# Rounding the weight pieces on ACT in the three projections with a convolution, DVE forming the remainders

## The reference, cut to what matters

```python
def causal_short_conv(x, w):
    s = x.shape[1]
    xp = jnp.pad(x, ((0, 0), (CONV_W - 1, 0), (0, 0)))
    y = xp[:, 0:s] * w[0]
    for k in range(1, CONV_W):
        y = y + xp[:, k:k + s] * w[k]
    return y
```

## Time and profile before

| | us |
|---|---|
| median of 3 runs | 5344.36 |
| lowest, highest | 5342.21, 5353.56 |
| profiled execution, its own time | 5340.43 |
| its span | 5338.6 |
| PE busy | 4357.7 (82%) |
| PEld busy | 2946.5 (55%) |
| DVE busy | 3132.0 (59%) |
| ACT busy | 731.9 (14%) |
| POOL busy | 818.7 (15%) |
| mean granted clock of TensorE | 0.909 of full speed |

### The profile page before, as it was taken

One profiled execution on the slowest core, in us unless ns is written; L12 is line 12 of the kernel. 1 busy time (PEld: TensorE's weight loads), 2 busy tenths in 40 slices (PEclk: granted clock), 3 DMA queues, 4 the chain that ended last, 5 costly groups with the idle time before them and its releaser, 6 DMA issues. The chain is left out here.

```text
span 5338.6 us, 46516 instructions
## 1 busy us (share of the span) xinstructions
PE 4357.7 (82%) x16256; PEld 2946.5 (55%) x16256; DVE 3132.0 (59%) x5411; ACT 731.9 (14%) x1680; POOL 818.7 (15%) x756
## 2 busy tenths in 40 slices
PE   7788969787787777677978678699996789787987
PEld 3676755222222222446746446577775567576876
DVE  2344357778778775654464485555556246445774
ACT  0111111111111010110131341100001210311000
POOL 1000023434433343100020041100002000001001
PEclk9899989999999999888989779799998699588998
DMA  7212216999999999200201101122222022022222
GB/s 252 85 56 81 88 63 260 423 424 423 423 416 416 415 416 421 76 24 8 75 16 64 49 1 53 60 87 89 91 90 68 24 75 80 8 73 74 95 77 75
DMA packets 212434, 813.26 MB, mean 152 GB/s; under 512 B 20288, under 2 KB 22608, under 8 KB 146448
## 3 DMA queue, kind: packets, MB, share of 16 engines
q0 software_dynamic: 73728, 536.90, 24.2%
q1 hardware_dynamic: 137408, 267.62, 15.1%
q10 hardware_dynamic: 1104, 6.30, 0.3%
HBM read 808.67 MB, written 2.10 MB: 152 GB/s over the span
## 5 line engine op out<-in xcount | busy, mean ns | idle before, releaser
L122 DVE CAST ring_high<-ring_raw 128x2048 fp32r<-128x2048 f32 (+2 forms) x250 | 274.4, 1097 | 934.7 <-PE psum L152 864.8
L150 PE MATMUL psum<-h_features,ring_high 128*128 128x512 f32 (+3 forms) x1432 | 566.0, 395 | 56.8 <-DVE ring_low L124 25.0
L151 PE MATMUL psum<-h_features,ring_high 128*128 128x512 f32 (+3 forms) x1432 | 562.4, 393 | 0.0
L152 PE MATMUL psum<-h_features,ring_low 128*128 128x512 f32 (+3 forms) x1432 | 562.0, 392 | 0.0
L124 DVE TENSOR_TENSOR ring_low<-ring_raw,ring_high 128x2048 fp32r<-128x2048 f32 (+2 forms) x250 | 509.6, 2038 | 19.0
L150 PE MATMUL psum<-ring_high,h_features 128*128 128x512 f32 x1120 | 443.1, 396 | 59.1 <-DVE ring_low L124 45.6
L925 PE MATMUL psum<-slots_ring,evacuation_tmp 128*128 128x512 f32 x816 | 403.7, 618 | 104.8 <-DVE evacuation_tmp L1023 104.7
L151 PE MATMUL psum<-ring_low,h_features 128*128 128x512 f32 x1120 | 441.0, 394 | 0.0
L152 PE MATMUL psum<-ring_high,h_features 128*128 128x512 f32 x1120 | 440.6, 393 | 0.0
L417 POOL TENSOR_SCALAR mean_var<-mean_var 128x1 f32<-128x1 f32 (+3 forms) x43 | 10.3, 241 | 2710.2 <-DVEq L455 1500.5
L925 PE MATMUL psum<-slots_features,evacuation_tmp 128*128 128x512 f32 x612 | 302.1, 617 | 77.2 <-DVE evacuation_tmp L1023 77.0
(11 more groups left out here) (453 smaller groups left out, 7227.0 us busy)
## 6 DMA issues: line engine op xcount, KB each, us to landing
ring_raw<-in_w_in SPq DMA_DIRECT2D x94, 1024.0 KB, 5.0
ring_raw<-in_w_gate_up SPq DMA_DIRECT2D x32, 1024.0 KB, 5.1
ada_ring<-in_w_ada SPq DMA_DIRECT2D x24, 1024.0 KB, 5.9
ring_raw<-in_w_up_pairs SPq DMA_DIRECT2D x20, 1024.0 KB, 4.9
ring_raw<-in_w_down SPq DMA_DIRECT2D x33, 512.0 KB, 3.6
ring_raw<-in_w_out SPq DMA_DIRECT2D x12, 1024.0 KB, 5.0
ring_raw<-in_w_down SPq DMA_DIRECT2D x10, 1024.0 KB, 4.9
ring_raw<-in_peer_w_q SPq DMA_DIRECT2D x8, 1024.0 KB, 5.1
```

Of the source, the lines that this page charges most:

```text
L122: nc.vector.tensor_copy(high, whole)
L150: nc.tensor.matmul(out, a[0], b[0], start=start, stop=False)
L151: nc.tensor.matmul(out, a[0], b[1], start=False, stop=False)
L152: return nc.tensor.matmul(out, a[1], b[0], start=False, stop=stop)
```

## The change

In a stage that has a "conv" run, the cast of every piece but the first ones (those of `split_first`) moves from DVE to ACT. ACT waits for what DVE waited for (`wait_piece`), copies raw to high and counts `rounded[half]`; DVE waits for that and forms the remainder. On ACT both roundings for chunk c + 1 stand ahead of ACT's work on chunk c. The stages get two semaphores more, all 24 of them. Other stages split as before.

```diff
--- before.py
+++ after.py
@@ -124,19 +124,48 @@
     return nc.vector.tensor_tensor(low, whole, high.bitcast(F32), ALU.subtract)
 
 
-def split_piece(nc, core, dve, c, half, cols=PIECE):
+def piece_columns(core, c, half):
 
     if isinstance(c, int):
         if c >= len(core.plan):
-            return
-        cols = core.plan[c][1][half].shape[1] * core.plan[c][1][half].shape[2]
-    dve.wait_ge(core.landed[half], 16 * (c + 1))
+            return 0
+        return core.plan[c][1][half].shape[1] * core.plan[c][1][half].shape[2]
+    return PIECE
+
+
+def wait_piece(core, eng, c, half):
+
+    eng.wait_ge(core.landed[half], 16 * (c + 1))
     if not isinstance(c, int) or c > 0:
         if half == 0:
-            dve.wait_ge(core.used, c)
+            eng.wait_ge(core.used, c)
         else:
-            dve.wait_ge(core.products, QUARTERS * c)
-    split(nc, dve, core.raw[:, half, 0:cols], core.high[:, half, 0:cols], core.low[:, half, 0:cols]).then_inc(core.split[half], 1)
+            eng.wait_ge(core.products, QUARTERS * c)
+
+
+def split_piece(nc, core, dve, c, half, cols=PIECE):
+
+    cols = piece_columns(core, c, half) if isinstance(c, int) else cols
+    if cols:
+        wait_piece(core, dve, c, half)
+        split(nc, dve, core.raw[:, half, 0:cols], core.high[:, half, 0:cols], core.low[:, half, 0:cols]).then_inc(core.split[half], 1)
+
+
+def round_piece(nc, core, act, c, half, rounded):
+
+    cols = piece_columns(core, c, half)
+    if cols:
+        wait_piece(core, act, c, half)
+        nc.scalar.copy(core.high[:, half, 0:cols], core.raw[:, half, 0:cols]).then_inc(rounded[half], 1)
+
+
+def rest_of_piece(nc, core, dve, c, half, rounded, number):
+
+    cols = piece_columns(core, c, half)
+    if cols:
+        dve.wait_ge(rounded[half], number)
+        nc.vector.tensor_tensor(core.low[:, half, 0:cols], core.raw[:, half, 0:cols], core.high[:, half, 0:cols].bitcast(F32),
+                                ALU.subtract).then_inc(core.split[half], 1)
 
 
 def split_first(nc, core, dve, start, first):
@@ -194,8 +223,9 @@
     start = plan_splits(core, 2 * core.taken + (2 if looped else 1))
     idle = lambda turn, odd: turn - (base + (base % 2 != odd)) // 2 + 1
     bank = lambda odd, t: core.ps[:, 4 * odd + t, :]
-    with stage(nc, name, "free0", "free1", "convolved", "loaded", "first_run", "var_ready", "root_ready") as (
-            block, free0, free1, convolved, loaded, first_run, var_ready, root_ready):
+    convolves = any(how[0] == "conv" for _, _, _, how in runs)
+    with stage(nc, name, "free0", "free1", "convolved", "loaded", "first_run", "var_ready", "root_ready", "rounded0", "rounded1") as (
+            block, free0, free1, convolved, loaded, first_run, var_ready, root_ready, *rounded):
         free = (free0, free1)
 
         if beside is not None:
@@ -251,9 +281,12 @@
                     dve.wait_ge(first_run, 1)
                     beside[1](dve, var_ready, root_ready)
                 for j, _, odd, c in pairs(dve, first, number):
-                    split_piece(nc, core, dve, c + 1, 0)
-                    if not isinstance(c, int) or c + 1 < core.taken:
-                        split_piece(nc, core, dve, c + 1, 1)
+                    for half in range(2):
+                        if half == 0 or not isinstance(c, int) or c + 1 < core.taken:
+                            if convolves:
+                                rest_of_piece(nc, core, dve, c + 1, half, rounded, c + 1 - base)
+                            else:
+                                split_piece(nc, core, dve, c + 1, half)
                     if how[0] == "act":
                         continue
                     for t in range(NT):
@@ -285,6 +318,9 @@
                     continue
                 rows = isinstance(layout, list)
                 for j, _, odd, c in pairs(act, first, number):
+                    for half in range(2):
+                        if convolves and (half == 0 or not isinstance(c, int) or c + 1 < core.taken):
+                            round_piece(nc, core, act, c + 1, half, rounded)
                     count = len(layout) if rows else NT
                     for t in range(count):
                         if how[0] == "conv":
```

## The result

The changed kernel takes 5358.18 us (median of 22 runs, 5348.48 to 5366.45), the kernel before 5345.79 (22 runs, 5331.10 to 5359.91, the three shown above among them). The ratio is 1.0018 with a 95% interval of 1.0011 to 1.0026: 9.6 us slower, between 5.9 and 13.9. On the three runs that stood ahead of the prediction that is 5354. The forecast was 4.8 slower, half of what came. The direction held. 5354 lies inside the whole range of 5341 to 5357, but above the forecast's own 5346.8 to 5353.2.

A forecast was written before the change was run, and what follows sets the result against it. PE was taken to bound `delta_in` and `mlstm_in`, with DVE level in `mamba_in`. Terms 3.3 + 1.05 + 0.45 gave 4.8 us slower, 5349.2; own range 5346.8 to 5353.2, whole range 5341 to 5357.

The forecast's parts named there:

- The mechanism forecast: In the three stages, ACT's first-half rounding queues behind a Silu awaiting DVE's last convolution: 1.05 us later; second half 0.70.
- neighbouring cases: Outcomes beside the forecast for the whole kernel; with them and the scatter of medians the range was 5341 to 5357.
- The rounding's length: On ACT, each full 128x2048 copy was taken to last 1.90 us, 2.2 at the dear end.
- +1.05 forecast: At the end of `delta_in`, DVE's remainder for the next stage stands behind the last Silu: 1.05 us slower.
- +0.45 forecast: In `mlstm_in`, 1.6 us later against slacks of 1.59 and 1.24: PE loses about 0.1 and 0.35.
- +3.3 forecast: In `mamba_in`, first and second halves' delays take turns without adding up fully; the stage ends 3.3 us later.
- its own sign of being right: Forecast wrong if `delta_in`, `mlstm_in` and `mamba_in` don't grow by about 1.0, 0.5 and 3.3 us.
- the walk turn by turn: In `mamba_in`, delays followed through each convolution and PE start: +0.70, +1.69, +0.68, +1.7, +2.2, +2.2, then +1.05 at the end.
- The table load: At eight late turns in the three stages, the copy forces a 1.28 us Silu reload: in all +15, 5359.5; chance 0.04.
- The clock's fall: PE's clock drops after all four longer holds, 2.1 us each: some +13, 5357.5; chance 0.06.
- The rival of a gain: DVE's freed time removes PE's holds in `mamba_in` and shortens last pieces: 5.5 us faster, 5338.9; chance 0.12.
- Semaphores: Every one of the 24 calls of `project` clears two more; taken as nothing, 0.8 us in all if priced like barrier events.

The follow-up runs named there:

- double_rounding: The changed kernel with every rounding on ACT done twice, a drain between; the three stages took 26.4 us more than in the changed kernel.
- first_half_ahead: The changed kernel with ACT's first-half rounding for chunk c + 2 moved ahead of the last Silu of chunk c; 1.0005 of the kernel before.
- mixed: The changed kernel with first-half roundings moved ahead of ACT's last Silu and second halves cast by DVE again; 1.0000 of the kernel before.
- late_only: The changed kernel with ACT rounding only in `mlstm_in` and `mamba_in`, `delta_in` splitting on DVE as before; 1.0009 of the kernel before.
- sems_only: The kernel before with only the two extra semaphores in each of the 24 stages, never used; 1.0006 of the kernel before.
- mixed_unrolled: The kernel mixed with the four convolved chunks of `mamba_in` written out instead of looped; 1.0000 of the kernel before.
- delta_only: The changed kernel with ACT rounding only in `delta_in`, the other two stages splitting on DVE as before; 1.0013 of the kernel before.
- before_unrolled: The kernel before with the four convolved chunks of `mamba_in` written out instead of looped; `mamba_in` took 105.90 us.
- after_unrolled: The changed kernel with the four convolved chunks of `mamba_in` written out instead of looped; `mamba_in` took 107.76 us.

## Why the prediction was right or wrong

**The view and the mechanism.** The mechanism forecast is the one the traces show in the three stages; that the 5354 still fell inside the whole range is owed to the room left there for neighbouring cases and scatter, since 3 of the 9.6 us come from outside the stages or from noise. PE bounds the first two stages, DVE stands level with it in the third, and the moved step sits behind a Silu: traces and double_rounding, first_half_ahead and mixed show it.

**Term by term.** The rounding's length: 1.90 forecast, 1.88 to 1.91 measured. `delta_in`: +1.05 forecast; +1.05 in the pair of first traces, 1.1 as the mean of three against two. `mlstm_in`: +0.45 forecast; at the same number of slow matmuls (7), 102.14 against 101.53, +0.6. `mamba_in`: **+3.3 forecast, +4.74 measured**. It had named about 3.3 here as its own sign of being right; the 1.4 over that are its largest miss inside the stages, and the step that fell short is the walk turn by turn. It had PE start 1.69 us later at the first turn; it was 1.94 (4499.30 against 4483.35, so 46.34 us into the stage against 44.40), after DVE had lost 0.36 to a longer issue gap between two convolution steps. At the loop's turn it had counted the loop and no table load; the load made the chain 1.28 longer. And it held PE's clock at full speed. late_only, with the load and without the longer gap and the fall, has +4.1: so of the 1.4 that were missing, 0.8 come with the load still there and the other two add 0.6. They don't add up fully, since a PE that is late itself hides part of the load's wait.

**The rivals.** The table load was a rival, at each of eight switches. It came at one, and for another reason than I had given. ACT's copy needs no load after a Silu (2250.83 and 4495.03 have none), as the Trainium skill (ScalarE: Activation LUTs, Table sets: the hidden batching unit) says of copies. The load comes at the head of the loop, 4516.46 (and once ahead of the loop, at the stage's start, where it costs nothing). The kernel before had its loop's load too, at each turn's first Silu, where DVE's next tile hid it. The changed one has both: the instruction at the head of the loop body was a Silu and is now a copy. I had read "3 loads in all" as no load at switches and had not asked why two of the three lay inside a loop. The clock's fall was a rival with four places at 2.1 us; it came at one place, after 2.25 us of hold, seven matmuls by 0.20, 1.4 us. By the idle times of the rows it came after 2.10 and not after 1.90 (4546.64), 1.79 (late_only, 4489.93) or 1.83 (before, at the stage's start). But the hold's length alone doesn't tell: in double_rounding a hold of 2.34 (4527.71) had no slower matmul behind it. I had worked out 1.8 for the hold, and left the case at 0.06. What decides the fall was not tested. The rival of a gain fell: no trace of the changed kernel has a stage shorter than before.

**What was counted at nothing.** Semaphores 0.5 us, inside the bounds given. DMA reloads and Silu's moved load: nothing, as said. What was missing altogether is the time outside the three stages. By traces the three stages cost 6.6 us (mean of three, 309.8, against mean of two, 303.2). The measured 9.6 leaves 3; since 6.6 lies inside its interval of 5.9 to 13.9, that pair alone doesn't show these 3 us. But all seven timed comparisons with the kernel before leave something on the same side. Time against three stages, us: the changed kernel 9.6 and 6.6, sems_only 3.2 and -0.1, first_half_ahead 2.7 and -2.1, mixed 0.0 and -3.8, mixed_unrolled 0.0 and -8.2, delta_only 7.0 and 1.1, late_only 4.8 and 4.2. The gap is 4.2 on average, each known to some 5 us either way, and several share their runs of the kernel before. All seven have the two semaphores, so a cost common to them outside the three stages, beyond the 0.5 us of the clears, stands as a rival that no run excludes. The traces neither show it nor rule it out: outside the three stages the three traces without the two semaphores spent 5032.8 to 5042.5 us, the eleven with them 5025.5 to 5048.1 (means 5037 and 5038). Inside that scatter the other candidate is the channel-decay stage, 10.4 us dearer in all three traces of the changed kernel and in delta_only, with the same instructions, at a lower granted clock.

**What stays open.** That stage's dearness is not settled as an effect of the change; the traces point both ways. Sorted by what stands ahead of the stage: the kernel before up to there (two traces of it, before_unrolled) 139.78, 139.78 and 136.53; the same with the two semaphores (sems_only, late_only) 142.14 and 140.10; the changed one up to there (three traces of it, delta_only, after_unrolled) 150.21, 150.14, 150.15, 150.20 and 138.17; mixed and mixed_unrolled, again alike up to there, 137.86 and 146.75. For an effect: four of the five with the changed code are at 150.2, and none of the five without roundings on ACT up to there is above 142.2. Against it: kernels with the same instructions up to that stage part by 9 and by 12 us, so the instructions alone don't decide it; double_rounding, whose `delta_in` is 10 us longer, has 138.08, and first_half_ahead, whose `delta_in` is shorter than before, 150.15.

What does go with the length is the clock at which the stage is entered. Its first 34 us, in the kernel before, the changed kernel and sems_only:

```profile
2693.54:2727.54 34.00, 17.83 (x84) 12.52 (x84) 24.56 (x44) 14.46 (x36) 10.91 (x9) 0.68 0.00 1
```

```profile
2694.12:2728.12 34.00, 17.48 (x62) 14.29 (x63) 19.78 (x39) 12.59 (x34) 7.79 (x6) 0.50 0.00 1
```

```profile
2689.32:2723.32 34.00, 17.83 (x63) 14.37 (x64) 19.78 (x39) 12.95 (x34) 7.79 (x6) 0.50 0.00 0
```

At a granted clock of 0.50, the lower level throughout, PE gets through 62 matmuls there, at 0.68 through 84. Of the 14 traces the seven that have 0.50 to 0.54 in these 34 us took 142.1 to 150.2 us for the stage, the seven that have 0.61 to 0.69 took 136.5 to 140.1. sems_only, which rounds nothing on ACT, enters as slowly as the changed kernel. What sets the clock at that point was not found, nor how often each case comes in executions without a trace, so I can't say how much of the 9.6 is this stage's share.

## What to carry to other kernels

Moving a step to an idle engine gains only if the step can run while that engine is idle: look at what stands ahead of it in that engine's order, and at who releases that. Here the same rounding, one place further up, turned 6.6 us of loss in the stages into 2.1 of gain, though no gain was measured in the whole time. Ask the same of hardware loops: what comes first in the body on ACT decides where a table load falls. And where PE's clock is in play, a few us saved in a stage of 100 are less than what a later stage with untouched instructions may differ by from one build to the next, here up to 13.7 us: compare stage by stage, and give the rest of the kernel its own line.

## What the runs showed of the hardware that I had not expected

A stage with 512 matmuls, its instructions untouched, took from 136.5 to 150.2 us by the kernel around it, with granted clocks from 0.86 to 0.77, and repeated to 0.1 us for the same kernel (139.78 twice; 150.21, 150.14, 150.15), while two kernels alike up to it took 137.86 and 146.75. A clear of a stage's semaphores takes about 0.02 us more for two more of them. With loop variables in their waits and addresses, the four convolution steps of a tile take 3.56 us from tile to tile in `mamba_in`; with constants they take 3.19, in `mlstm_in` and in before_unrolled's `mamba_in` alike. That is 0.37 us a tile, 5.9 us of DVE's time over 16 tiles, about as much as the 6.6 us that the change cost in the three stages.
